# Two 1 MB gate and up loads per list in place of four of 512 KB, in the expert tiles of a two-layer transformer step

## What is computed

```
gate = jnp.einsum('td,edf->tef', t, w_gate_l)      # D = 1024, f = 256
up = jnp.einsum('td,edf->tef', t, w_up_l)
act = jax.nn.silu(gate) * up * combine[..., None]
return jnp.einsum('tef,efd->td', act, w_down_l)
```

## Time and profile before

| | us |
|---|---|
| median of 3 runs | 1941.95 (1940.6 to 1942.61) |
| the profiled execution | 1943.26, its span 1941.2 |
| TensorE matmuls, busy | 1726.5 (89%) |
| mean granted TensorE clock | 0.957 |
| gate and up products (line 2422) | 209.3 busy, 36.0 idle ahead of them |
| down products (line 2435) | 110.7 busy, 21.2 idle ahead of them |

### The profile page before, as it was taken

One profiled execution on the slowest core, in us unless ns is written; L12 is line 12 of the kernel. 1 busy time (PEld: TensorE's weight loads), 2 busy tenths in 40 slices (PEclk: granted clock), 3 DMA queues, 4 the chain that ended last, 5 costly groups with the idle time before them and its releaser, 6 DMA issues. The chain is left out here.

```text
span 1941.2 us, 34689 instructions
## 1 busy us (share of the span) xinstructions
PE 1726.5 (89%) x13363; PEld 1351.5 (70%) x13363; DVE 957.3 (49%) x1849; ACT 718.6 (37%) x1394; POOL 501.9 (26%) x268
## 2 busy tenths in 40 slices
PE   5999999989999987788689998888899999588893
PEld 4899866679999974222188997567899998432222
DVE  4285476785667333111283744766766652611114
ACT  4443465553433421111254434656433342211113
POOL 1303410065456302000101123201545551200004
PEclk8999999999999988999789999999999999899996
DMA  7512377823522337987442221001232340889744
GB/s 275 195 44 68 106 249 248 275 94 129 192 91 88 143 143 298 360 303 261 143 147 98 67 67 36 1 2 44 66 98 66 98 145 21 354 311 393 278 136 174
DMA packets 170647, 305.95 MB, mean 158 GB/s; under 512 B 12530, under 2 KB 123250, under 8 KB 169716
## 3 DMA queue, kind: packets, MB, share of 16 engines
q1 hardware_dynamic: 151248, 249.09, 37.1%
q10 hardware_dynamic: 13476, 33.67, 4.8%
q0 software_dynamic: 5760, 20.97, 2.9%
HBM read 517.87 MB, written 41.68 MB: 288 GB/s over the span
## 5 line engine op out<-in xcount | busy, mean ns | idle before, releaser
L2422 PE MATMUL psum<-xw,h_T 128*32 128x512 f32 x1792 | 209.3, 611 | 36.0 <-DMA xw<-w_expert 32.4
L181 PE MATMUL psum<-whi,h_hi 128*128 128x256 f32 x720 | 210.1, 292 | 0.5 <-ACT v_tok L1011 0.5
L817 POOL TENSOR_TENSOR wlo<-raw,whi 128x2048 fp32r<-128x2048 f32 x25 | 115.2, 4608 | 362.3 <-ACT whi L897 362.3
L181 PE MATMUL psum<-whi,h_lo 128*128 128x256 f32 x720 | 203.5, 283 | 0.0
L181 PE MATMUL psum<-wlo,h_hi 128*128 128x256 f32 x720 | 203.5, 283 | 0.0
L2422 PEld LDWEIGHTS psum<-xw,h_T 128*32 128x32 f32 x1792 | 53.9, 111 | 170.5 <-issue 113.5
L977 ACT ACTIVATE prob<-psum,small_stats 128x640 f32<-128x640 f32 (+1 forms) x160 | 112.0, 705 | 134.5 <-DVE small_stats L1380 134.3
L1380 DVE TENSOR_REDUCE small_stats<-psum 128x1 f32<-128x640 f32 (+1 forms) x160 | 107.3, 712 | 96.7 <-PE psum L1684 72.2
L2319 DVE TENSOR_TENSOR gated_x<-psum,sig_x 128x256 f32<-128x256 f32 x28 | 11.9, 425 | 279.9 <-ACT sig_x L2066 279.9
L181 PEld LDWEIGHTS psum<-whi,h_hi 128*128 128x128 f32 x720 | 137.5, 191 | 3.0 <-issue 1.8
L181 PEld LDWEIGHTS psum<-wlo,h_hi 128*128 128x128 f32 x720 | 137.9, 192 | 0.0
(11 more groups left out here) (375 smaller groups left out, 4108.3 us busy)
## 6 DMA issues: line engine op xcount, KB each, us to landing
xw<-w_expert SPq DMA_DIRECT2D x672, 512.0 KB
raw<-w_in SPq DMA_DIRECT2D x46, 1024.0 KB, 5.4
wm_rest<-w_mod SPq DMA_DIRECT2D x40, 1024.0 KB, 5.3
y_rows<-y_sel ACTq DMA_DIRECT2D x108, 128.0 KB, 5.2
h_sel<-h_rows ACTq DMA_DIRECT2D x22, 512.0 KB, 6.9
wm<-w_mod SPq DMA_DIRECT2D x4, 2048.0 KB, 16.1
raw<-w_out SPq DMA_DIRECT2D x8, 1024.0 KB, 5.2
h_rows<-c_zero ACTq DMA_DIRECT2D x4, 1536.0 KB, 8.9
```

Source lines behind the costliest of these rows:

```text
L181: mm = pe.matmul(dst, st, mv[q], start=start and n == 0, stop=stop and n == 2)
L817: pool.tensor_tensor(wlo[i % 2][:, :, :], raw[i % 2][:, :, :], whi[i % 2][:, :, :].bitcast(F32), ALU.subtract).then_inc(w_lo, 1)
L2422: mm = pe.matmul(psum[list_rows(q), i % 2, :], hT[i % 2][:, kc, q, :], xw[q][c][:, k * 512:(k + 1) * 512], start=(kc == 0), stop=(kc == KD ...
```

## The change

The four loads of the parts of one list become two, each of two parts (1 MB, a pattern of 128 partitions by 2 by 1024 with two pieces of 4 KB for each partition). SP waits for two parts of the product before it issues four of them, and reads two list entries behind each four. TensorE waits ahead of part 0 and part 2 only, on two semaphores instead of four; the threshold is `i + 2`, since the first loads, which stay as they were, now bring twice the count on each of the two. The buffers lie where they lay.

```diff
--- before.py
+++ after.py
@@ -482,7 +482,10 @@
 
 
         xw_at = ((48, 52, 64, 68, 72, 76), (16, 20, 24, 28, 32, 36), (40, 44, 80, 84, 56, 60), (88, 92, 96, 100, 104, 108))
-        xw = [[at(f"xw{q}_{c}", [P, D], Z + off * K) for c, off in enumerate(offs)] for q, offs in enumerate(xw_at)]
+        assert all(offs[c + 1] == offs[c] + 4 for offs in xw_at for c in (0, 2))
+        xw_two = [[at(f"xw{q}_parts{c}", [P, 2, D], Z + offs[2 * c] * K) for c in range(2)] for q, offs in enumerate(xw_at)]
+        xw = [[xw_two[q][c // 2][:, c % 2, :] if c < N_PARTS else at(f"xw{q}_{c}", [P, D], Z + off * K) for c, off in enumerate(offs)]
+              for q, offs in enumerate(xw_at)]
         hT = [at(f"h_T{i}", [P, KD, N_LISTS, SLOT], (20 + 4 * i) * K) for i in range(2)]
         h_sel = [at(f"h_sel{i}", [P, D], (28 + 4 * i) * K) for i in range(2)]
         aT = [at(f"act_T{i}", [P, 2, P], (36 + i) * K) for i in range(2)]
@@ -1953,8 +1956,8 @@
                         v = sp.value_load(slot_i[0:1, q, s:s + 1], min_val=0, max_val=2 * NE - 1)
                         return v % NE, v < NE
 
-                    def load_part(c, q, expert, cond):
-                        sp.dma_start(xw[q][c][:, :], w_exp[c, expert, :, :], cond=cond,
+                    def load_two(c, q, expert, cond):
+                        sp.dma_start(xw_two[q][c][:, :, :], w_exp[2 * c:2 * c + 2, expert, :, :].rearrange("c p d -> p c d"), cond=cond,
                                      bounds_check="skip_entire_dma").then_inc(xw_ld[c], 16)
 
                     def load_down(h, q, expert, cond):
@@ -1971,13 +1974,13 @@
 
                     sp.wait_ge(g_pfree, 24)
                     for c in range(N_PARTS):
-                        sp.dma_start(xw[0][c][:, :], w_exp[c, 0]).then_inc(xw_ld[c], 16)
+                        sp.dma_start(xw[0][c][:, :], w_exp[c, 0]).then_inc(xw_ld[c // 2], 16)
                     sp.wait_ge(o_full, KD)
                     sp.dma_start(routes[:, :], a["c_route"].partition_broadcast(P)).then_inc(r_c, 16)
                     low_ready(sp, N_STREAM - 1)
                     for c in range(N_PARTS):
                         for q in range(1, N_LISTS):
-                            sp.dma_start(xw[q][c][:, :], w_exp[c, PER_LIST * q]).then_inc(xw_ld[c], 16)
+                            sp.dma_start(xw[q][c][:, :], w_exp[c, PER_LIST * q]).then_inc(xw_ld[c // 2], 16)
                     for q in (0, 1, 3):
                         first_down(q)
                     sp.wait_ge(k_d, TT)
@@ -1992,12 +1995,12 @@
                     for i in range(N_TILES):
                         nxt = []
                         if i + 1 < N_TILES:
-                            for c in range(N_PARTS):
-                                sp.wait_ge(x_pt, N_PARTS * i + c + 1)
+                            for c in range(2):
+                                sp.wait_ge(x_pt, N_PARTS * i + 2 * c + 2)
                                 for q in range(N_LISTS):
-                                    load_part(c, q, *ahead_of[q])
+                                    load_two(c, q, *ahead_of[q])
                                 if i + 2 < N_TILES:
-                                    nxt.append(list_load(i + 2, c))
+                                    nxt += [list_load(i + 2, q) for q in (2 * c, 2 * c + 1)]
                         if i >= 1:
                             for h in range(2):
                                 sp.wait_ge(x_dn, 2 * i - 1 + h)
@@ -2416,8 +2419,8 @@
                             pe.wait_ge(x_ac, i - 1)
                         for kc in range(KD):
                             c, k = divmod(kc, KD // N_PARTS)
-                            if k == 0:
-                                pe.wait_ge(xw_ld[c], 16 * N_LISTS * (i + 1))
+                            if k == 0 and c % 2 == 0:
+                                pe.wait_ge(xw_ld[c // 2], 16 * N_LISTS * (i + 2))
                             for q in range(N_LISTS):
                                 mm = pe.matmul(psum[list_rows(q), i % 2, :], hT[i % 2][:, kc, q, :], xw[q][c][:, k * 512:(k + 1) * 512],
                                                start=(kc == 0), stop=(kc == KD - 1))
```

## The result

The change makes the kernel **slower by 1.1%**: 1960.66 us (median of 4 runs, 1960.08 to 1964.32) against 1941.36 for the kernel before beside it, a ratio of 1.011 with a 95% interval of 1.0094 to 1.0127. That is +19.3 us where +4.4 was forecast, and 0.7 us beyond the range (1930 to 1960). The rival in which both the tail and the later trigger count had given +20.3. The profiled execution of the changed kernel took 1960.08, its span is 1958.0, 16.8 more than before.

A forecast was written before the change was run, and what follows sets the result against it. TensorE was taken as the bound, busy 1726.5 of 1941.2 us, with DMA the limit around loading tiles and SP nearly as full. Terms: 15.9 - 9.1 - 4 + 1.6 = +4.4, giving 1946.4 us; range 1930 to 1960.

The forecast's parts named there:

- The rival in which both the tail and the later trigger count: Gate and up loads: DMA runs dry between tiles, so both delays cost, 31.8 us; sum +20.3, 1962 us; chance 0.14.
- term 1: Nine tiles loading two or three lists: 32 matmuls follow the last bytes, +15.9 us; 0 to 31.8 with the later trigger.
- term 4: TensorE's clock: fewer, longer waits bring one more fall to half clock, +1.6 us, from 0 to 8.
- terms 2 and 3: SP's queue: eight fewer issues a tile make gate and up loads land earlier, -9.1 us, and down loads leave earlier, -4.
- term 2: Gate and up loads in seven two-list tiles: last half lands 1.3 us earlier, -9.1 us; between 0 and 7 x 2.4 = -16.8.
- the two signs of an error: Wrong if each layer's twelve tiles get shorter by over 5 us, or, second, if the half-clock stretches multiply.
- SP was the limit: SP's issuing at line 1957 limits two-list tiles, so halving the issues gains: -14.4 us, 1927.6 us; chance 0.22.
- larger transfers run faster: Weight loads: fewer 1 MB transfers save fixed time that stood on the path, -9 us, 1933 us; chance 0.06.

The follow-up runs named there:

- the tail alone: Kernel before, quarters loaded as before, but TensorE waits for both quarters of a half at a time: 1952.34 us, ratio 1.0073.
- with SP relieved: SP waits for two quarters, in the kernel before without skipped issues and their list reads: 1940.37 us, 14.9 above the same without the later wait.
- packing: Kernel before, with a tile's four list entries packed by VectorE into one integer that SP reads at once: 1932.51 us, ratio 0.9963.

## Why the prediction was wrong

**The step that failed** is in term 1: "I take the single count, since now SP is mostly late anyway". The tail's size was near: +15.9 against 12.8 measured alone (11.6 to 16.7 by its interval). That is in part luck: the 15.9 were to be delay alone, and of the 11.5 us that the tiles grew by with the tail alone 5.2 are idle time and 6.3 the clock, of which term 4 had only 1.6. The trigger was set to nothing, and is worth 17.9 alone (15.9 to 24.1), 14.9 with SP relieved. Together they gave 34.2, just above the upper end that I had kept, 31.8. With the tail and the trigger as measured together and the other terms as they stand, the sum is 34.2 - 9.1 - 4 + 0 = +21.1 (the clock is in the 34.2), between the 19.3 and the 27.0 measured.

Two things were misread. The lateness of SP was rightly seen: it has 52 such waits in each layer and stood in 15 of the first layer's and in 3 of the second's, 18.8 us in all. But I took "mostly late" for "late by more than a quarter". Asked to wait for the second quarter, SP stood 22 of 52 times, for 38.6 us. There it may have been late for the first quarter's end, but it was early for the second's. Even in tile 1, which I read this from, SP was through at 764.9, and the second quarter's last matmul ended at 765.1, not at 764.7: its product had started at a lower clock. The other misreading: I priced one quarter at 1.77 us, the time of its matmuls. In a burst TensorE itself waits between two quarters (1.85 us in the tile above), and the second quarter's end is later by that too. The reason I gave for the rival, that DMA runs dry, fits what was measured: without the skipped issues the trigger costs 14.9 us, and in the changed kernel the DMA share is 0.57 while the last half runs. By how much the dry stretches of all bursts add up was not measured.

**SP's relief** (terms 2 and 3, -13.1) can't be called wrong: the change gives back 7 to 15 us of the 34. That leaving out the skipped issues and their reads gave 13.1 as well is no check of it, since it is another relief. Of the down loads, TensorE's waits fell from 11.6 to 9.0 us, 2.6 against the 4 taken. How the rest divides between issues and bytes was not separated. The 2.4 us behind the far end of term 2 are not worked out there, and no run gives them.

**The clock** (term 4) was mis-sized: +1.6 taken, with 8 as the upper end; the busy time of the tiles rose by 7.2. I counted one more fall to half clock. What the earlier trace rows shows repeats: behind 9 of the 19 waits for gate and up weights the 32 matmuls took 5.1 to 6.6 us instead of 3.64. Before, 4 of 23 waits were followed by matmuls at less than full clock.

**What would show it.** Right were the 208 issues for loads of 1 MB, the place of the waits (ahead of matmul 1 and 33), and SP's waiting. The waits themselves range from 0.25 to 5.7 us, 10 of the 19 within the 2 to 5 foreseen. Tile 2's last half came at 781.46, just behind the 779 to 781. Of the two signs of an error the second came: the half-clock stretches multiplied. The DMA share of the full stretches of the second layer stayed near 0.9:

```profile
1717.00:1770.00 53.00, 44.47 (x362) 14.44 (x354) 6.29 (x11) 7.23 (x13) 0.00 (x0) 0.90 0.92 342
1770.00:1822.00 52.00, 41.45 (x318) 13.72 (x318) 5.23 (x9) 6.85 (x12) 0.00 (x0) 0.87 0.92 357
```

**The rivals.** That SP was the limit had a true half: it is on the path (0.42 us for each added read, -6.4 from packing), but the change takes from its relief by letting the loads start later. That larger transfers run faster isn't shown: quarters with both waits merged and halves of 1 MB differ by 4 us within overlapping intervals, and the DMA engines' busy time in the tiles of the changed kernel did not fall. The Trainium skill (DMA: Bandwidth & Descriptors, section Bandwidth) would have transfers batched to 1 MiB or more; in this trace the granularity of the waits around them decided against it. That both tail and trigger count, given 0.14, is what happened. Given that nothing was worked out on how late SP was, it deserved more.

## What to carry to other kernels

Before merging loads into a single buffer, count two delays: the consumer starts later by the added work behind the last byte, and the load starts later by the time until the larger piece is free. Here they added (12.8 and 17.9 alone, 34.2 together), and the second grows where the consumer itself waits between the two pieces. A producer queue that is late for one piece isn't safe from a later trigger: compare how late it is with the time to the end of the next piece. Where a DMA queue's issuing is on the path, take work from the queue (fewer register reads, fewer skipped issues) and leave the grain of the loads as it is, above all that of the last piece.

## What was not expected of the hardware

A wait of 3 to 5 us ahead of a product could cost 2.2 to 3.0 us more in the clock. After 5.12 us of waiting 32 matmuls took 5.80 us, after 4.47 they took 6.32, after 3.35 they took 6.61, where 3.64 are their time at full clock. It isn't so each time: this half waited for 3.38 us and ran at full clock.

```profile
1849.41 3.64 PE L2425 MATMUL psum<-xw_parts,h_T 128*32 128x512 f32 x32 [3.38 <-DMA xw_parts<-w_expert]
```

Over the tiles, 7.2 of the 20.8 us that they grew by are clock, not waiting.

A load of twice the size costs SP little more to issue. The DMA instructions of the changed line in 768 to 790 us, around tile 2's burst (ns min/median/max, first and last start), skipped and real ones:

```profile
L1960 SPq DMA_DIRECT2D xw_parts<-w_expert x11: 73/387/391, 768.3 to 789.0; - x11
```

A real one takes some 390 ns here against some 340 before, a skipped one 73 at the least, as before. And the read of one list entry, an instruction that looks free in TensorE's view, was worth 0.42 us of the kernel's time each when 104 were added.
